# The last gate-up multiplies each high weight tile by both halves of the token tile in one 512-column product, and VectorE adds the two bank halves

## The reference, cut to what matters

```
gate = rmsnorm(h, g) @ w_gate        # 256 x 1024 times 1024 x 2816
up   = rmsnorm(h, g) @ w_up
h    = h + 0.5 * ((silu(gate) * up) @ w_down)
```

## Time and profile before

| | us |
|---|---|
| three runs | 964.58, 965.96, 970.26 |
| median | 965.96 |
| the profiled execution's own time | 967.7 |
| its span in the trace | 965.9 |
| TensorE busy | 951.5 (99%) |
| VectorE busy | 639.9 (66%) |
| ScalarE busy | 494.6 (51%) |

### The profile page before, as it was taken

One profiled execution on the slowest core, in us unless ns is written; L12 is line 12 of the kernel. 1 busy time (PEld: TensorE's weight loads), 2 busy tenths in 40 slices (PEclk: granted clock), 3 DMA queues, 4 the chain that ended last, 5 costly groups with the idle time before them and its releaser, 6 DMA issues.

```text
span 965.9 us, 19407 instructions
## 1 busy us (share of the span) xinstructions
PE 951.5 (99%) x7543; PEld 883.8 (92%) x7543; DVE 639.9 (66%) x995; ACT 494.6 (51%) x762; POOL 68.7 (7%) x100
## 2 busy tenths in 40 slices
PE   8999999999999999999999999999999999999997
PEld 3776778899999999899999999999999999999997
DVE  4788886687666765765555546665778766666554
ACT  4765647664454543554444434645665554444531
POOL 0012002200000021000000000200210100000000
PEclk9999999999999999999999999999999999999999
DMA  9972447546666795266666744663445557667741
GB/s 359 400 259 89 131 133 241 185 162 198 183 187 182 207 303 152 67 196 176 179 181 178 224 119 125 214 187 109 129 135 168 160 177 215 188 181 208 220 137 43
DMA packets 189183, 176.06 MB, mean 182 GB/s; under 512 B 7312, under 2 KB 177824, under 8 KB 188752
## 3 DMA queue, kind: packets, MB, share of 16 engines
q1 hardware_dynamic: 183456, 154.29, 52.8%
q0 software_dynamic: 4960, 17.64, 5.2%
q10 hardware_dynamic: 720, 3.49, 0.9%
HBM read 174.32 MB, written 1.05 MB: 182 GB/s over the span
## 4 chain that ended last, share of the span: by engine, by line
PE 85%; DVE 9%; ACT 3%; issue 1%; DMA 1%; SPq 1%; DVEq 0%; ACTq 0%
PE acc L2007 24%; PE acc L2009 23%; PE acc L2008 23%; DVE lo L1143 2%; PE acc L2400 1%; DMA slab_hi<-in_w_ada 1%; PE acc L2205 1%; ACT hi L621 1%; PE acc L2207 1%; PE acc L2206 1%; PE wk L2007 1%; PE acc L2136 1%; PE wk L2009 1%; PE wk L2008 1%; PE wk L2136 1%
## 5 line engine op out<-in xcount | busy, mean ns | idle before, releaser
L1143 DVE TENSOR_TENSOR lo<-raw,hi 128x1024 fp32r<-128x1024 f32 (+1 forms) x259 | 331.0, 1288 | 209.4 <-ACT hi L621 209.1
L621 ACT ACTIVATE hi<-raw 128x1024 fp32r<-128x1024 f32 (+1 forms) x260 | 283.2, 1098 | 130.2 <-PE acc L2009 125.3
L2007 PE MATMUL acc<-n_high,hi 128*128 128x272 f32 (+3 forms) x1016 | 291.2, 287 | 0.5 <-DVE n_low L1958 0.3
L2008 PE MATMUL acc<-n_low,hi 128*128 128x272 f32 (+3 forms) x1016 | 288.1, 284 | 0.0
L2009 PE MATMUL acc<-n_high,lo 128*128 128x272 f32 (+3 forms) x1016 | 288.0, 283 | 0.0
L2007 PEld LDWEIGHTS acc<-n_high,hi 128*128 128x128 f32 (+1 forms) x1016 | 191.7, 189 | 3.0 <-issue 1.4
L2008 PEld LDWEIGHTS acc<-n_low,hi 128*128 128x128 f32 (+1 forms) x1016 | 191.3, 188 | 0.5
L2009 PEld LDWEIGHTS acc<-n_high,lo 128*128 128x128 f32 (+1 forms) x1016 | 191.3, 188 | 0.2
L2007 PE MATMUL acc<-g_high,hi 128*128 128x256 f32 (+1 forms) x528 | 149.2, 283 | 0.0
L2009 PE MATMUL acc<-g_high,lo 128*128 128x256 f32 (+1 forms) x528 | 148.9, 282 | 0.0
L2008 PE MATMUL acc<-g_low,hi 128*128 128x256 f32 (+1 forms) x528 | 148.7, 282 | 0.0
(11 more groups left out here) (428 smaller groups left out, 1246.1 us busy)
## 6 DMA issues: line engine op xcount, KB each, us to landing
raw<-in_w_in SPq DMA_DIRECT2D x52, 512.0 KB, 4.1
raw<-in_w_ffn_in SPq DMA_DIRECT2D x44, 512.0 KB, 3.7
raw<-in_ffn_w_gate SPq DMA_DIRECT2D x44, 512.0 KB, 3.8
raw<-in_ffn_w_up SPq DMA_DIRECT2D x44, 512.0 KB, 3.8
raw<-in_ffn_w_down SPq DMA_DIRECT2D x32, 704.0 KB, 4.5
stage<-in_w_late POOLq DMA_DIRECT2D x24, 512.0 KB, 4.8
raw<-in_w_ffn_out SPq DMA_DIRECT2D x16, 704.0 KB, 5.9
raw<-in_w_out SPq DMA_DIRECT2D x16, 512.0 KB, 4.2
```

The lines of the kernel that those rows point to most:

```text
L621: act.activation(hi[:, j, 0:width], raw[:, j, 0:width], ACT.Copy).then_inc(hi_ready, 1)
L1143: dve.tensor_tensor(lo[:, j, 0:width], raw[:, j, 0:width], hi[:, j, 0:width].bitcast(F32), ALU.subtract).then_inc(lo_ready, 1)
L2007: pe.matmul(out_, wH, xH, start=start, stop=False)
L2008: pe.matmul(out_, wH, xL, start=False, stop=False)
```

## The change

The token parts become one tensor `mix`, `[P, 2, KD, T]`, with `mixH` and `mixL` as views of it. For the last gate-up, `split_mm2` replaces `split_mm`. It multiplies the high weight tile by both token parts in one product of 512 columns. The high tokens' result falls into columns 0 to 255 of the bank and the low tokens' into columns 256 to 511. Then it adds low weights by high tokens, 256 columns, into columns 0 to 255. VectorE gets a `tensor_reduce` for each bank pair, which reads all 1024 columns of two banks and adds the halves into 512. The multiplications that read the accumulator before now read the sum in SBUF. They wait for it through the semaphore `hb_ready`. The banks are still freed by the multiplication.

```diff
-        mixH = sbuf(root, "mixH", [P, KD, T], F32R)
-        mixL = sbuf(root, "mixL", [P, KD, T], F32R)
+        mix = sbuf(root, "mix", [P, 2, KD, T], F32R)
+        mixH, mixL = mix[:, 0], mix[:, 1]
...
+            def gate_up_twin(name, f, ahead):
+                def evac(i, j):
+                    if j == 1:
+                        multiplied(name, i, j)
+                        src = first_pair(i)
+                        dve.tensor_reduce(sg[:, :, 0:T], src.rearrange("p m (h t) -> p m t h", h=2), mybir.AxisListType.X, ALU.add).then_inc(hb_ready, 1)
+                        dve.wait_ge(hb_ready, COUNT["gu0"] + 2 * i + 1)
+                        dve.tensor_tensor(sg[:, :, 0:T], sg[:, :, 0:T], tokens_inv(T), ALU.mult).then_inc(acc_free[0], 1)
+                    if j == 3:
+
+                        multiplied(name, i, j)
+                        dve.wait_ge(lo_ready, 4 * (BASE[name] + i) + 5)
+                        dve.tensor_reduce(hbuf[:, :, 0:T], acc[:, 2:4, :].rearrange("p m (h t) -> p m t h", h=2), mybir.AxisListType.X, ALU.add).then_inc(hb_ready, 1)
+                        dve.wait_ge(hb_ready, COUNT["gu0"] + 2 * i + 2)
+                        dve.wait_ge(sg_ready, COUNT[name] * f + i + 1)
+                        dve.tensor_tensor(hbuf[:, :, 0:T], hbuf[:, :, 0:T], sg[:, :, 0:T], ALU.mult).then_inc(acc_free[1], 1)
+                        dve.wait_ge(gh_ready, COUNT[name] * f + i + 1)
+                        dve.tensor_tensor(inner(g_low, T)[:, ds(2 * i, 2), :], hbuf[:, :, 0:T],
+                                          inner(g_high, T)[:, ds(2 * i, 2), :].bitcast(F32), ALU.subtract).then_inc(gl_ready, 1)
+                pipeline(name, 1024, evac, ahead, peel=True, behind=((0,), (), (), (1, 2, 3)))
...
-            gate_up_scaled("gu2", 2, T, DN)
+            gate_up_twin("gu2", 2, DN)
...
+            def split_mm2(out_, wH, wL, xs, start, stop):
+
+                pe.matmul(out_, wH, xs, start=start, stop=False)
+                return pe.matmul(out_[:, 0:T], wL, xs[:, 0], start=False, stop=stop)
...
+                def twin(i, s, use):
+
+                    set_free(s, use)
+                    for q in range(2):
+                        j = 2 * s + q
+                        arrived(g + i, j)
+                        for kk in range(4):
+                            k = 4 * q + kk
+                            for m in range(2):
+                                w = slice(256 * kk + P * m, 256 * kk + P * m + P)
+                                ins = split_mm2(acc[:, 2 * s + m, :], hi[:, j, w], lo[:, j, w], mix[:, :, k, :], k == 0, k == KD - 1)
+                        ins.then_inc(mm_done, 1)
...
-            gate_up("gu2", 0, T, lambda: sum_squares(6, T), 41, HALVES, (mixH, mixL))
+            gate_up_twin("gu2", lambda: sum_squares(6, T), 41)
```

More of the change, by code:

```diff
@@ L2450, in _, with gate_up_twin @@
             HALVES = [(4 * q + kk, s) for q in range(2) for s in range(2) for kk in range(4)]
+            def gate_up_twin(name, behind, first):
+                g = BASE[name]
+                outs = (wk[:, 1, :], wk[:, 2, :], acc[:, 2, :], acc[:, 3, :])
+                for k, s in HALVES:
+                    if (k, s) == (0, 1):
+                        set_free(1, USE[name])
+                    if (k, s) == (4, 1):
+                        behind()
+                    arrived(g, 2 * s + k // 4)
+                    pe.wait_ge(nl_ready, first + k + 1)
+                    for m in range(2):
+                        j, w = 2 * s + k // 4, slice(256 * (k % 4) + P * m, 256 * (k % 4) + P * m + P)
+                        ins = split_mm2(outs[2 * s + m], hi[:, j, w], lo[:, j, w], mix[:, :, k, :], k == 0, k == KD - 1)
+                    if (k, s) in ((3, 0), (KD - 1, 0), (4, 1), (KD - 1, 1)):
+                        ins.then_inc(mm_done, 1)
[6 more added lines that the diff above has]
+                            k = 4 * q + kk
+                            for m in range(2):
+                                w = slice(256 * kk + P * m, 256 * kk + P * m + P)
+                                ins = split_mm2(acc[:, 2 * s + m, :], hi[:, j, w], lo[:, j, w], mix[:, :, k, :], k == 0, k == KD - 1)
+                        ins.then_inc(mm_done, 1)
+                twin(1, 0, USE[name])
+                twin(1, 1, USE[name] + 1)
+                with pe.Fori(2, COUNT[name]) as i:
+                    for s in range(2):
+                        twin(i, s, USE[name] + i)
             def gate_up(name, t0, width, behind, first, steps, operands=(mH, mL)):
```

## The result

| | before | after |
|---|---|---|
| median of five runs, us | 965.96 | 978.96 |
| lowest and highest | 964.58, 970.26 | 975.99, 981.05 |
| the profiled execution's own time | 967.7 | 977.36 |
| its span | 965.9 | 975.6 |
| from the last norm to the end norm | 177.44 | 188.55 |

The changed kernel is slower: ratio 1.0133, interval 1.0113 to 1.0154, so 11 to 15 us. The prediction was 975.7, range 966 to 981. It runs from the start of VectorE's reciprocal for the last gate-up (781.56 before, 780.09 after) to the start of its small reciprocal in the closing norm (959.00, 968.64). It holds nearly all of what the change touches and leaves out differences elsewhere in the kernel.

A forecast was written before the change was run, and what follows sets the result against it. TensorE bounded the kernel before; with the reductions, VectorE and ScalarE's closed ring would. Start 3.5, eight turns 4.7, last turn 0.2 and down product 1.24 made 9.7 us: 975.7 against the median, range 966 to 981.

The forecast's parts named there:

- the ring: VectorE and ScalarE passing work to and fro in the last gate-up: 9.42 us a turn, 11.90 with two reductions.
- the last turn: Last gate-up's final turn: up banks come free about 0.3 us too late, the turn takes 11.5, costing 0.2 us.
- Rival A: VectorE's reduction is paced by its 512 results, 0.71 us each: ring 10.84, 967.6 us, not slower; chance 0.13.
- rival B: VectorE's reduction at scan pace or paying for short runs, 2.29 us: 998 us; chance 0.11 including anything between it and forecast.
- The gate link: VectorE, from the gate reduction to the multiplication waiting for it: 1.24 us added to each turn.
- The up link: VectorE, from the up reduction to the multiplication waiting for it: 1.24 us added to each turn.
- TensorE's turn: TensorE's products in one last gate-up turn: 32 pairs of 0.350 us, 11.2 us in place of 11.31.
- the start: Last gate-up: three reductions lie ahead of the gate banks coming free, so TensorE starts turn 2 3.5 us late.
- eight turns: Turns 2 to 9 of the last gate-up: period 11.90 against 11.31, costing 4.7 us.
- the down product: Its second quarter waits for `lo[1]` without slack, and one more reduction lies ahead: 1.24 us.
- Rival C: TensorE's idle pieces of 0.7 us lower its granted clock; given almost nothing as chance.
- The estimate of 10.4 us a turn: TensorE's last gate-up turn by the skill's formula, N/2.4 + 2.5 ns: 32 times (216 + 109) ns.

The follow-up runs named there:

- The reductions alone: The changed kernel with its reductions kept, but three products of 256 columns again, the second into columns 256 to 511: 978.05 us, ratio 1.0143.
- the late silu: The changed kernel with reductions kept, but from turn 1 on ScalarE makes hi[2] before the silu of sg: 974.09 us, ratio 1.0098.
- early banks: The changed kernel, but from turn 1 on TensorE takes banks back after the reduction (`hb_ready`), not after the multiplication: 978.13 us, ratio 1.0149.
- The dose of 0.68: The changed kernel with each reduction replaced by a copy of columns 0 to 255, low tokens' product left out: 970.35 us, ratio 1.0068.
- the written-out kernel: The kernel before the change, with TensorE's turns 2 to 10 of the last gate-up written out instead of looped: 968.78 us, ratio 1.0046.

## Why the prediction was right, and where it was off

**The mechanism** was right: the ring of 9.42, two reductions in it, TensorE overtaken and idle for 0.7 us in each turn. The reductions alone reproduce the loss, the late silu takes the period back to 11.3, and early banks don't. One thing was placed wrongly. The prediction put the whole 0.7 ahead of quarter 0. It stands in two places, 0.45 before the gate pair and 0.29 before the up pair, the 0.3 that the prediction had reckoned for the last turn alone.

**The reduction**, 1.21 expected from the copy row, is 1.218. Rival A (0.71) and rival B (2.29) fall with it. The dose of 0.68 shows what A would have looked like: no loss per turn, 2.5 us in all.

**The ring** was mis-sized by 0.13: 12.03 in place of 11.90. The gate link is 1.26 where 1.24 was expected. The up link is 1.34. With copies in place of the reductions the same two links were 0.71 and 0.81, so the extra tenth does not depend on the length of what stands before. The program has two things more in the up link: a `REGISTER_ALU` between the reduction and the wait, and a second wait, for the silu. The prediction named register work as a cost that would only add and gave it no price. Which of the two takes the extra 0.1 was not tried apart.

**TensorE's turn** was put at 11.2 and is 11.3. A pair costs 0.353 and not 0.350 (a wide product 0.235 and not 0.232), so the wide product gains nothing. Since the ring was longer than either, this changed no term.

**The sum.** In the stretch, from turn start to turn start: the start 3.7 (predicted 3.5), eight turns 5.7 (4.7), the last turn 0.4 (0.2), the down product 1.3 (1.24). Together 11.1, against 9.7 predicted. The two profiled executions differ by 977.36 - 967.7 = 9.7 as wholes, but that agreement is luck. Outside the stretch the profiled run of after was 1.4 us quicker, and of the earlier down product it shows x443 where before shows x427, with nothing changed there.

**The medians** differ by 13.0, so the prediction was 3.3 short. Of that 1.4 is the ring and its kin above. The other 1.9 is not from the change's steps: the profiled run of before lay 1.7 above its median and that of after 1.6 below its own, less the 1.4 outside the stretch. A likely reason, which no run settles: both profiles of the kernel before caught the slow pace in its loop (177.4), while a quick one makes 173.6. Its other runs can use a quick pace. The changed kernel gains nothing from one, since the ring holds it. Against a quick loop the loss in the stretch would be 15 us. The measured interval of 11 to 15 does not decide between the two.

**Rival C**: the granted clock was 1.00 in the stretch and 0.998 over the span, as before. No sign of it, though TensorE paused in every turn.

**The estimate of 10.4 us a turn**, worked out from the issue gap in the Trainium skill (TensorE: Matmul & The Clock Gate, Back-to-back issue gap), fails here: the turn is 11.3. I had also used the formula where it isn't meant: the same section of the Trainium skill gives it for a matmul by itself, and for a stream of weight loads and matmuls some 131 ns at 512 columns. The 0.235 us of this trace agrees with neither. The advice of the Trainium skill against tensor_reduce on a hot path (VectorE: DVE Perf Modes, Rules for kernel authors) was right in direction. Its 1x mode by elements read fits the trace: 1.218 us for 1024 elements, beside 1.228 for a subtraction of 1024.

## What to carry to other kernels

Where two helper engines pass work to and fro, find a turn in which they catch up, read its length from start to start, and compare that with the period of the engine that bounds. The difference is all that may be added in a turn: here 1.89 us, where an addition of 1.52 cost no turn anything (2.5 us in all, at the start and the end) and one of 2.60 cost 0.7 in every turn. And one wide product in place of two narrow ones saved instructions here, but no columns and no time. It pays for nothing that must be added elsewhere.

## What the hardware showed that I had not expected

- Products of 256 columns have two paces, 0.1133 and 0.1177 us from start to start, at a granted clock of 1.00. In stretches of up to a thousand starts without a gap the pace stayed, but for one spot in the written-out kernel, where six products in a row were slow. Otherwise it changed only at a wait, a gap or the entry of a loop. In the kernel with the reductions alone, TensorE had one or the other from one wait to the next. The same program showed x427 and x444 in the same 50 us of two executions.
- Pairs of 512 and 256 columns showed one pace alone in all runs, 0.353, which is three times 0.1177.
- A reduction of 1024 elements to 512, read from two PSUM banks with a stride of 256 within each sum, costs 1.22 us, as much as an elementwise instruction on 1024 elements (1.228 in the earlier trace rows).
